# Later read-back of the state-space tiles, and a projection loop that takes the attention halves of two column blocks before their state-space halves

## The reference, cut to what matters

```
q, k, v, u, g_na, g_ssm = split(rms_norm(h) @ w_in)
y_na  = neighbourhood_attention(q, k, v, rpb) @ w_proj_na
y     = gelu(s5_forward(u) + s5_backward(u) + u * d_skip)
y_ssm = (y * sigmoid(y @ w_glu)) @ w_proj_ssm
mixed = sigmoid(g_na) * y_na + sigmoid(g_ssm) * y_ssm
h = h + mixed @ w_out
h = h + conv_gated_ffn(rms_norm(h), w_up, conv_w, conv_b, w_down)
out = rms_norm(h)[:, 16:]
```

## Time and profile before

| | before |
|---|---|
| median of 3 runs | 1491.97 us (1491.43 to 1492.33) |
| span of the profiled execution | 1488.4 us |
| median of the runs less this span | 3.6 us |
| PE busy | 1460.3 us (98%) |
| POOL, ACT, DVE busy | 1052.9, 672.6, 593.9 us |
| read from HBM | 263.32 MB |

### The profile page before, as it was taken

The page is one execution under the profiler, slowest core; times in us unless marked ns, Lnnn a source line. Parts: engine busy times, 40 slices in busy tenths (PEclk is TensorE's granted clock), DMA queues, the critical chain, the costliest instruction groups (busy, mean ns, idle before and its releaser), DMA issues.

```text
span 1488.4 us, 30666 instructions
## 1 busy us (share of the span) xinstructions
PE 1460.3 (98%) x11826; PEld 1387.4 (93%) x11826; DVE 593.9 (40%) x1151; ACT 672.6 (45%) x913; POOL 1052.9 (71%) x496
## 2 busy tenths in 40 slices
PE   8999999999999999999999999999999999999997
PEld 7999999998888899999999999999999998888886
DVE  3766788888556334443322222222222222003002
ACT  6446444431335464444554444444444443334333
POOL 5400038873578678888788888888888887888885
PEclk9999999999999999999999999999999999999999
DMA  7897457653576455575555565555555555555553
GB/s 221 288 223 216 134 159 220 197 177 93 153 229 210 152 169 170 183 257 178 177 185 184 183 184 183 183 183 182 181 182 181 182 182 197 193 185 184 191 189 129
DMA packets 250494, 277.14 MB, mean 186 GB/s; under 512 B 30748, under 2 KB 236924, under 8 KB 249772
## 3 DMA queue, kind: packets, MB, share of 16 engines
q1 hardware_dynamic: 235840, 254.84, 56.2%
q10 hardware_dynamic: 14508, 21.09, 4.3%
q0 software_dynamic: 64, 0.07, 0.0%
HBM read 263.32 MB, written 12.39 MB: 185 GB/s over the span
## 4 chain that ended last, share of the span: by engine, by line
PE 80%; DVE 10%; DVEq 2%; issue 2%; DMA 2%; ACT 2%; SPq 1%; POOL 0%; ACTq 0%
PE ps L1538 20%; PE ps L1540 20%; PE ps L1539 20%; PE ps L1907 6%; PE ps L1906 6%; PE ps L1908 6%; DVE ps L1065 3%; DVE scan_states L1254 3%; DVEq L1253 2%; DMA w_raw<-in_w_in 1%; PE ps L1748 1%; DVE t L1065 1%; SPq L462 1%; ACT w_hi L520 1%; DVE w_lo L524 1%
## 5 line engine op out<-in xcount | busy, mean ns | idle before, releaser
L524 POOL TENSOR_TENSOR w_lo<-w_raw,w_hi 128x1024 fp32r<-128x1024 f32 x425 | 1023.2, 2414 | 398.8 <-ACT w_hi L520 257.5
L520 ACT ACTIVATE w_hi<-w_raw 128x1024 fp32r<-128x1024 f32 x464 | 490.2, 1060 | 677.7 <-PE ps L1540 492.8
L1538 PE MATMUL ps<-act_hi,w_hi 128*128 128x258 f32 (+2 forms) x2432 | 696.4, 286 | 1.0 <-DVE act_lo L1006 1.0
L1540 PE MATMUL ps<-act_hi,w_lo 128*128 128x258 f32 (+2 forms) x2432 | 691.8, 284 | 0.0
L1539 PE MATMUL ps<-act_lo,w_hi 128*128 128x258 f32 (+2 forms) x2432 | 691.2, 284 | 0.0
L1538 PEld LDWEIGHTS ps<-act_hi,w_hi 128*128 128x128 f32 x2432 | 463.0, 190 | 6.1 <-issue 4.4
L1539 PEld LDWEIGHTS ps<-act_lo,w_hi 128*128 128x128 f32 x2432 | 463.4, 191 | 0.0
L1540 PEld LDWEIGHTS ps<-act_hi,w_lo 128*128 128x128 f32 x2432 | 462.0, 190 | 0.0
L1906 PE MATMUL ps<-w_hi,hidden_hi 128*128 128x512 f32 x352 | 139.2, 395 | 0.0
L1908 PE MATMUL ps<-w_lo,hidden_hi 128*128 128x512 f32 x352 | 139.0, 395 | 0.0
L1907 PE MATMUL ps<-w_hi,hidden_lo 128*128 128x512 f32 x352 | 139.0, 395 | 0.0
(11 more groups left out here) (268 smaller groups left out, 1563.3 us busy)
## 6 DMA issues: line engine op xcount, KB each, us to landing
w_raw<-in_w_up SPq DMA_DIRECT2D x176, 512.0 KB, 3.5
w_raw<-in_w_in SPq DMA_DIRECT2D x128, 512.0 KB, 4.1
w_raw<-in_w_down SPq DMA_DIRECT2D x88, 512.0 KB, 3.9
w_raw<-in_w_out SPq DMA_DIRECT2D x32, 512.0 KB, 3.4
w_raw<-in_w_proj_na SPq DMA_DIRECT2D x16, 512.0 KB, 3.4
w_raw<-in_w_proj_ssm SPq DMA_DIRECT2D x16, 512.0 KB, 3.3
w_raw<-in_w_glu SPq DMA_DIRECT2D x8, 512.0 KB, 3.5
bias_rows<-skew_scratch ACTq DMA_DIRECT2D x24, 128.0 KB
```

What stands on the lines that cost most here:

```text
L520: act.activation(slot(whi, k), slot(raw, k), ACT.Copy).then_inc(s_hi, 1)
L524: pool.tensor_tensor(slot(wlo, k), slot(raw, k), slot(whi, k).bitcast(F), ALU.subtract).then_inc(s_lo, 1)
L1538: mm(o, slot(whi, k)[:, cols], xh[:, kt, lo:lo + n], start=kt == 0, stop=False)
L1540: ins = mm(o, slot(wlo, k)[:, cols], xh[:, kt, lo:lo + n], start=False, stop=kt == units * UKT - 1)
```

## The change

Two edits.

**Read-backs.** The first four `y_load` calls leave the part of SP's stream that stores the tiles; all eight now stand behind every second unit of sixteen (units 40 to 55 of the gates), where four stood behind each of units 40 to 43. ACT's `y_order` moves from iteration 3 to the end of iteration 5, DVE's `gelu_lo` from iteration 4 to 6.

**Projection loop.** In each iteration PE takes the attention halves of both column blocks (four units), waits for `z_lo`, and takes the state-space halves of both (four units). The weight loads follow that order. DVE mixes block 0 after six units of the iteration and block 1 after eight, where it was four and eight. ACT's and POOL's streams in this loop are as they were.

```
@@ SP
             for t in range(KH):
                 load_in(U_G, 4 * HALF, 4, (t,))
                 y_store(t)
-                if 0 < t < 5:
-                    y_load(t - 1)
...
-            for u in range(4):
-                load_in(U_G, 4 * HALF, 5, (u,))
-                y_load(KH - 4 + u)
-            load_in(U_G, 4 * HALF, 5, range(4, 8))
-            with sp.Fori(6, 8) as i:
-                load_in(U_G, 4 * HALF, i)
+            for u in range(16):
+                load_in(U_G, 4 * HALF, 5 + u // 8, (u % 8,))
+                if u % 2 == 1:
+                    y_load(u // 2)
+            load_in(U_G, 4 * HALF, 7)
...
-                    w = (w_proj_na, w_proj_ssm)[k % 4 // 2]
-                    load(U_PROJ + 8 * i, k, kblock(w[0], i * (2 * CB) + (k // 4) * CB, k % 2))
+                    w = (w_proj_na, w_proj_ssm)[k // 4]
+                    load(U_PROJ + 8 * i, k, kblock(w[0], i * (2 * CB) + (k % 4 // 2) * CB, k % 2))
@@ ACT
-                    if b == 3 and n == 2:
+                    if b == 5 and n == 3:
                         y_order()
@@ DVE
-                if b == 4:
+                if b == 6:
                     dve.wait_ge(s_ygh, 1)
...
-                    dve.wait_ge(s_used, 8 * i + (U_PROJ + 4 * (k + 1)))
+                    dve.wait_ge(s_used, 8 * i + (U_PROJ + 6 + 2 * k))
@@ PE
             with pe.Fori(0, 4) as i:
                 for k in range(2):
                     pe.wait_ge(s_mx, 4 * i + (2 * k - 2 + SEED))
-                    product(U_PROJ + 8 * i, 4 * k, 2, anh, anl, 0, NL, (4 * k, 4 * k + 1))
-                    pe.wait_ge(s_zl, KH)
-                    product(U_PROJ + 8 * i, 4 * k + 2, 2, zh, zl, 0, NL, (4 * k + 2, 4 * k + 3))
+                    product(U_PROJ + 8 * i, 2 * k, 2, anh, anl, 0, NL, (4 * k, 4 * k + 1))
+                pe.wait_ge(s_zl, KH)
+                for k in range(2):
+                    product(U_PROJ + 8 * i, 4 + 2 * k, 2, zh, zl, 0, NL, (4 * k + 2, 4 * k + 3))
```

## The result

The changed kernel takes 1494.68 us (median of 20 runs), the kernel before 1491.57 us (median of 20 beside them): a ratio of 1.0020, with a 95% interval of 1.0012 to 1.0027. It is slower by about 3.0 us, and the interval, 1.8 to 4.0 us, straddles the 0.2% that I had set as the bound. The two profiled spans are 6.5 us apart, twice that, so the first thing to read is where each span got its time.

The account below looks back on a forecast made before the run. The prediction took PE, busy for 98% of the span, to bound the kernel. Its terms, -2.9 (read-backs) - 2.04 (`z_lo`) + 3.7 (`w_lo` waits) + 1.4 (projection's end), gave +0.2 us: 1492.1 us, range 1488.5 to 1495.5.

Parts of the forecast that it names:

- `z_lo`, -2.04 us: Projection: PE wants `z_lo` two units later, so its wait is hidden, -2.04 us.
- Four waits for `w_lo`, +3.7 us: End of each projection iteration: ACT rounds block 0's tiles before unit 8, so PE waits 0.93 us, +3.7 us in all.
- No wait for `mix_made` in the changed kernel: Ahead of block 1's attention units: additions end at 5.0 us, PE comes at 5.74, so no wait.
- The end, +1.4 us: Start of the output projection: the second `mixed_lo` subtraction waits for POOL until about 9.9 us, PE wants it at 8.6.
- The sum of the loop: Projection loop and its end: -2.04 us won, +3.7 and +1.4 us lost.
- Read-backs, -2.9 us: Attention: PE's waits for q, k, v and the scores' eviction fall from 5.0 to 2.1 us, bounds -3.6 and 0.
- With 8 us to landing: Load of unit 44 in the attention: lands 8 us after issue, between medians of 6.1 and 10.6 us.
- The prediction's own sign of being wrong: Profile of the attention: a wait for v or for `w_raw` between 410 and 460 us would show the forecast wrong.
- The waits for the scores, 1.8 to 2.1 us in all: Attention: eviction waits of about 0.2, 0.5, 0.7 and 0.7 us at pairs 3 to 6, none at pair 7.
- the read-backs do not help: Rival on the attention: landings stay near 10.6 us, the -2.9 become 0, 1495.0 us; chance 0.16.
- The first rival: Projection loop: ACT and POOL have unit 8 ready in time, both losses fall away, 1487.0 us; chance 0.12.
- The second: Rival on the projection loop: block 0's additions meet POOL, +3.1 us per iteration, 1495.2 to 1504.5 us; chance 0.12.

Follow-up runs that it names:

- E2: The kernel before with only the read-backs' new places and the moved `y_order` and `gelu_lo`, projection loop as before: 1492.25 us, ratio 1.0004.
- E5: The kernel before with only the last four read-backs spaced, one behind every second load, `y_order` in its old place: 1488.88 us, ratio 0.9981.
- E7: The kernel before with only `y_order` moved to ACT's iteration 5 and `gelu_lo` to DVE's iteration 6: 1492.76 us, ratio 1.0010.
- E11: The kernel before, unchanged, in one more profiled execution: attention 123.70 us, projection 94.24 us.
- E3: The changed kernel with ACT rounding two weight units ahead of block 0's tiles, and a PE wait ahead of the output projection: 1490.95 us, ratio 0.9999.
- E4b: The changed kernel without any read-back, the reorder reading another tile of the same size: 1493.44 us, ratio 1.0010.
- E8: E3 with PE waiting in the projection loop for the multiplications that last read the banks, not for the additions: 1489.18 us, ratio 0.9982.
- E12: The changed kernel, unaltered, in one more profiled execution: attention 123.61 us, projection 95.67 us.
- E9: The kernel before with the projection loop of E8 and the spaced read-backs of E5: 1486.25 us, ratio 0.9961.
- E1: The kernel before with only the projection loop's new order, read-backs as before: 1492.88 us, ratio 1.0009.
- E10: The kernel before with only the projection loop of E8: 1487.64 us (seven runs), ratio 0.9975.

## Why the prediction was right in part

The forecast was 1492.1 us, range 1488.5 to 1495.5; the median is 1494.68. The sum was +0.2 us, the measured difference is +3.0 (1.8 to 4.0). The time lies in the range only because the range was wide enough to hold a read-back edit that wins nothing; the loop's terms were right by their mechanism. By its steps:

- **`z_lo`, -2.04 us: right.** The wait is gone in every loop with the new order and stays in E2, E5, E7 and E11.
- **Four waits for `w_lo`, +3.7 us: right in place, size and cause.** From start to start the projection grew by 1.41 us, and 2.31 of the `z_lo` wait had gone: 3.72 for four, 0.93 each (the prediction's own steps, added up, give 0.96). The profile prints 0.61 to 0.72, since it counts idle time from the modelled end of the last matmul. They are 23.97 us apart (forecast 23.9), the last at the first `mixed_hi`. The step-by-step sum held too: additions of 0.77 us with POOL idle, and 560.73 + 1.06 + 0.07 + 2.4 + 0.12 = 564.4 for PE's 564.30. E3 shows that ACT's order is the cause.
- **No wait for `mix_made` in the changed kernel: right**, but E3 shows how thin it was: where PE comes 0.9 us earlier, the same additions of block 1 (4.3 us) make it wait 0.57 us.
- **The end, +1.4 us: right.** The two subtractions end 10.2 us after the start of the output projection (forecast 9.9), the wait is 1.41 us, and the stage is 1.78 longer.
- **The sum of the loop: +3.06 forecast, +3.19 measured.**
- **Read-backs, -2.9 us: this is the step that failed; measured 0, or a small loss.** The issue came earlier as forecast (4.0 us, with 3.5 to 5.5 expected). "With 8 us to landing" was wrong: it took 11, as before, so ACT rounded unit 44 at 33.7 us behind the scores of pair 0, not at 31 to 32. And "they land by 428 to 430", that is by 37.8 to 39.8 us on this scale, was wrong as well: with 6.7 us for the last of them they let PE start at 41.8, where it wanted them at 41.0. The wait at pair 3 shrank by 2.4 us in this execution, but pairs 2, 4 and 5 wait 1.6 us together, and over five executions the waits for v went from 3.8 to 3.0 us: 0.8 won where 3.2 were forecast. The prediction's own sign of being wrong, a wait for v between 410 and 460 us, is there. E4b shows that the read-backs lengthen the landings (10.8 against 6.7 us for the median of three), but also that 8 us for unit 44 was short even without them (8.8 us).
- **The waits for the scores, 1.8 to 2.1 us in all: wrong, and in the first trace right in size (1.9) by luck.** Over the five executions the waits for DVE are 2.9 us, from 1.5. "The wait at pair 7 should vanish" came true in none of the five in effect: in the first L1361 met the next full operation of POOL there (2.90 us) and PE waited 1.15 us (E2: 1.18), and where the gate was free (E3, E8, E12) the scalings met POOL and the transposes waited 1.24 to 2.02 us. The term had held the move of `y_order` to be free, and E7 shows that it isn't. The 0.2, 0.5, 0.7 and 0.7 us at pairs 3 to 6 came in one execution of the five (E12: 0.63 to 0.69 at each). The forecast of a phase half a microsecond wide could not be had from the trace of another kernel, as E5 and E9, equal in this code, show.

The rival that was right is the third, *the read-backs do not help*, at 1495.0 us, right in its sum; but pair 3 did not wait as before, the waits for v spread out and those for DVE grew. Its long landings came: beside read-backs with rows of 272 B the loads took 10.8 us to land, without them 6.7. The Trainium skill, page "DMA: Bandwidth & Descriptors", section "Specifications", says that a transfer needs 512 B to run at full rate. That would fit, but no run here varied the size of a row, and it could as well be that more transfers stood in the queues; which it is stays open. The first rival, that ACT's order doesn't bite, is refuted by E1 and E3. The second, that the additions meet POOL, did not happen in the first half of any iteration, and E3 made it happen. My -2.9 went by the earlier issue; the landing was an unknown with rows at 6.1 and 10.6 us, and nothing in the change took away what made it 10.6.

E5 has a timed gain of 2.8 us where the change has none. It differs from the change in two things at once, four tiles inside the attention instead of eight and `y_order` in its old place. E7 puts a price on the second in PE's waits, but is itself timed at +1.5 us with an interval of -0.1 to 3.3, and no run has the new read-backs with `y_order` in its old place, nor could one, since it needs all of them. Nor do the traces account for all of E5's gain: PE idles 3.1 and 5.2 us in the attention of E5 and E9, against a mean of 5.2 with the old read-backs.

What I can't settle is the last microsecond: stage by stage the edits give +3.2 us and the timed interval is 1.8 to 4.0, but E1 alone was timed at +1.3 (-0.1 to 2.8) for its +3.17, and E10 at -3.7 (-5.2 to -2.1) for its -2.0. The attention and the start scatter by as much in each execution.

## What to carry to other kernels

When work moves to another place in PE's stream, move the in-order streams that prepare the next units along with it: ACT's order was left as it was, and the 2.3 us won were paid for with 5.5. Make the semaphore say what the waiter needs (the bank has been read) and not what comes after it (the sum is made). Before you count an earlier issue as a gain, ask whether what made the transfer slow has moved as well. And read a stage that scatters from several executions: the waits for DVE in the attention of one kernel were 1.9 us in one and 4.0 us in another.

## What the hardware showed that I had not expected

**The clock fell at some waits of 1.2 to 3.4 us, and at others of the same length it did not.** Windows of 10 us (the column behind POOL's is the granted clock), of the changed kernel and of E11:

```profile
500.00:510.00 10.00, 8.85 (x65) 7.99 (x64) 3.93 (x11) 4.14 (x12) 7.35 (x4) 0.83 0.57 184
```

```profile
430.00:440.00 10.00, 7.40 (x52) 6.38 (x53) 6.37 (x9) 5.30 (x13) 10.00 (x9) 0.83 0.65 194
```

Behind the wait of 1.15 us at 501.55, matmuls start 0.215 us apart instead of 0.12 for some 3.4 us, that is at the 1.2 GHz level, and then at 2.4 again. It costs about 1.7 us. In the first execution of before PE idled 3.19 us at 433.86 and the clock stayed at 1.00; in E11, the same code, it idled 3.37 us there and the clock fell. The attention less PE's idle time in it is 116.6 to 117.1 us in the eight executions whose clock stayed up, 118.0 to 118.3 us in the four with one such stretch (changed, E1, E3, E11), and 119.5 us in E10, where it lasted 6.8 us. So 122.5 = 116.6 + 5.9 before, and 123.6 = 116.6 + 5.3 + 1.7 in the changed kernel. E7 had its stretch behind the `z_lo` wait, and its projection took 95.69 us instead of 94.25. In these six of the thirteen executions a wait thus cost more than its length.

**The start varies with the clock too.** Over the first 50 us the granted clock was 0.93 in both executions of before and 0.86 in both of the changed kernel, whose code there is the same; their stage ahead of the attention was 388.8 and 390.3 us against 392.6 and 394.5. Other kernels with the changed read-backs began as early as before (E3 390.19, E8 389.19, E4b, which has none, 389.10), so the 2.3 us are not the change's; what made the clock differ is not shown.

**An operation with one SBUF tile also stands behind POOL.** The four scalings of the scores (L1329, a tile and a column of factors) take 0.97 us together where POOL is idle and 6.69 us beside it. The Trainium skill, page "SBUF — State Buffer", section "Who interferes with whom", says that such an operation can run in a fast mode that takes both port pairs of DVE, one of them shared with GpSimd, and that whichever of the two engines issues first then blocks the other. The rows agree with that; which mode the operation ran in they don't show. I had watched only the operations with two SBUF inputs.
